# Unread products, count products and weight splits moved in the routing and last stages of a one-layer encoder

## The reference

```python
x = layer_norm(ALPHA * x + a, lp['ln1_g'], lp['ln1_b'])                       # a: token mixing
x = layer_norm(ALPHA * x + cross_attend(x, mk, mv, lp['w_xq'], lp['w_xo']), lp['ln2_g'], lp['ln2_b'])
x = layer_norm(ALPHA * x + hier_moe(x, lp), lp['ln3_g'], lp['ln3_b'])
...
def cross_attend(x, mk, mv, w_xq, w_xo):
    ...
    return o @ w_xo                                                            # the outward product
...
def hier_moe(x, lp):
    logits_g = (xt @ lp['w_router_group']).astype(jnp.float32) + lp['b_router_group'].astype(jnp.float32)
    ...
    top_v, top_i = lax.top_k(le, TOP_K)
    gate = (jax.nn.softmax(top_v, axis=-1) * pg[:, None]).reshape(-1)
    ...
    h = jax.nn.silu(xb @ w_g[e]) * (xb @ w_u[e])                               # one block of rows of expert e
    return (h @ w_d[e]) * wts[:, None].astype(xt.dtype)
```

## Time and profile before

| | us |
|---|---|
| median of 3 timed runs | 1626.03 |
| lowest, highest | 1622.83, 1627.28 |
| profiled execution | 1628.42 |
| its span (first to last instruction) | 1625.8 |
| PE busy | 1552.3 (95%) |
| DVE busy | 1005.0 (62%) |
| ACT busy | 787.0 (48%) |
| POOL busy | 362.8 (22%) |
| mean granted TensorE clock | 0.978 |

### The profile page before, as it was taken

How to read it: one execution, slowest core, us unless ns; L and a number is a source line. 1 busy time by engine, 2 the same in 40 slices (tenths; PEclk the granted TensorE clock), 3 DMA queues, 4 the chain that set the end, 5 groups by cost and what they waited for, 6 DMA issues and landing times.

```text
span 1625.8 us, 21437 instructions
## 1 busy us (share of the span) xinstructions
PE 1552.3 (95%) x8440; PEld 1279.9 (79%) x8440; DVE 1005.0 (62%) x1282; ACT 787.0 (48%) x1143; POOL 362.8 (22%) x277
## 2 busy tenths in 40 slices
PE   8999999999988999999999988999999999999966
PEld 6877887677766888999777777888888888888842
DVE  5611111777644655222555458989889998999936
ACT  5411121555454013222422234887888887888834
POOL 0000000477862851000122111131111121111005
PEclk9999999999999999999999977999999999999987
DMA  9721111600333545000445536999999999999876
GB/s 356 260 76 39 43 56 59 174 23 19 118 104 132 184 170 193 27 21 1 156 156 175 175 130 251 385 368 396 387 382 399 398 389 393 385 392 398 342 283 282
DMA packets 86331, 352.69 MB, mean 217 GB/s; under 512 B 23512, under 2 KB 28248, under 8 KB 64474
## 3 DMA queue, kind: packets, MB, share of 16 engines
q1 hardware_dynamic: 76106, 331.41, 54.1%
q0 software_dynamic: 9216, 18.89, 3.0%
q10 hardware_dynamic: 912, 1.05, 0.2%
HBM read 321.93 MB, written 43.15 MB: 225 GB/s over the span
## 4 chain that ended last, share of the span: by engine, by line
PE 85%; DVE 5%; DMA 4%; ACT 3%; issue 1%; POOL 0%; SPq 0%; DVEq 0%; POOLq 0%; ACTq 0%
PE M L1348 23%; PE M L1067 12%; PE T L862 6%; PE M L835 6%; PE T L1348 5%; PE T L771 3%; DMA beside<-in_w_exp_up 3%; DVE rounded L1905 3%; PE M L771 3%; PE M L950 2%; PE T L1409 2%; PE T L1139 2%; PE T L1137 2%; PE T L1138 2%; PE M L1171 2%; PE M L1153 2%
## 5 line engine op out<-in xcount | busy, mean ns | idle before, releaser
L1905 DVE TENSOR_TENSOR rounded<-beside,rounded 128x1024 fp32r<-128x1024 f32 (+1 forms) x397 | 471.4, 1233 | 57.2 <-ACT rounded L1791 46.7
L1348 PE MATMUL M<-rounded 128*128 128x512 f32 x1908 | 461.3, 392 | 2.8 <-ACT rounded L1826 1.9
L1348 PEld LDWEIGHTS M<-rounded 128*128 128x128 f32 x1908 | 355.8, 188 | 77.7 <-ACT rounded L1826 2.1
L1791 ACT CAST rounded<-beside 128x1024 fp32r<-128x1024 f32 x256 | 258.9, 1050 | 80.9 <-DMA beside<-in_w_exp_up 75.4
L1067 PE MATMUL M<-rounded 128*128 128x512 f32 x816 | 196.7, 395 | 2.9 <-ACT rounded L1661 1.7
L1067 PEld LDWEIGHTS M<-rounded 128*128 128x128 f32 x816 | 150.1, 188 | 33.9 <-issue 2.0
L1801 ACT CAST rounded<-beside 128x1024 fp32r<-128x1024 f32 x128 | 125.2, 1049 | 24.2 <-DMA beside<-in_w_exp_down 22.3
L2573 POOL DMA_INDIRECT expert_rows<-beside,route_out x32 | 41.8, 1305 | 394.8 <-ACT beside L1832 389.5
L2506 POOL TENSOR_SCALAR arena<-arena,rinv 128x384 f32<-128x384 f32 (+7 forms) x64 | 110.2, 1726 | 48.9 <-DVE rinv L2033 48.7
L1348 PE MATMUL T<-rounded 128*128 128x512 f32 x384 | 108.7, 398 | 0.0
L1905 DVE TENSOR_TENSOR rounded<-T,rounded 128x512 fp32r<-128x512 f32 (+2 forms) x84 | 79.0, 944 | 20.7 <-ACT rounded L1674 17.7
(11 more groups left out here) (374 smaller groups left out, 2462.4 us busy)
## 6 DMA issues: line engine op xcount, KB each, us to landing
beside<-in_w_exp_gate SPq DMA_DIRECT2D x64, 1024.0 KB, 8.1
beside<-in_w_exp_up SPq DMA_DIRECT2D x64, 1024.0 KB, 10.9
beside<-in_w_exp_down SPq DMA_DIRECT2D x32, 2048.0 KB, 11.4
arena<-x_rows SPq DMA_DIRECT2D x27, 512.0 KB, 3.7
x_rows<-arena SPq DMA_DIRECT2D x18, 512.0 KB, 3.1
arena<-expert_rows SPq DMA_DIRECT2D x9, 1024.0 KB, 12.7
arena<-in_x_prompt SPq DMA_DIRECT2D x16, 512.0 KB, 3.9
arena<-in_cache_mem_k SPq DMA_DIRECT2D x8, 1024.0 KB, 5.7
```

Of the source, the lines that this page charges most:

```text
L1348: got = nc.tensor.matmul(out, x[xs], (high, low)[ws](w)[:, c:c + 512], start=(first and n == 0), stop=(last and n == 2))
L1791: nc.scalar.copy(as_both(high(c)), both_raw(c)).then_inc(gu_high, 1)
L1905: return nc.vector.tensor_tensor(out, x, highs.bitcast(f32), ALU.subtract)
```

## The change

Six edits, all between the last outward product and the experts, and at the start of the last stage:

1. On PE the samples' outward product is cut into parts: `samples_high` (high rows by both weight parts) for four chunks of the first half ahead of `turn_x2(PT - 1)`, four behind it, the second half's behind `route_rows(PT - 1)`, and the low products (`samples_low`) last. `turn_memory_rows(NB - 1)` goes ahead of them. On ACT `turn_x2(PT - 1)` goes behind `out_high(PT)`. The samples' low part is made by DVE and no longer by POOL.
2. For the last prompt tile DVE adds the epsilon of the norm, and POOL only takes the inverse root.
3. DVE sums the eight pick tables into `picked` (the buffer of `r_end`), and one product each takes the place of the 16 count products; they stand behind later waits.
4. Nine unread f32 products (`ident` by `tables`, 512 columns) stand behind the ranks, four unread rounded ones behind the slot products, and 26 instead of 20 behind the totals.
5. The splits of the first expert's weights on DVE: chunk 0 goes behind the prompt tiles' slots, chunks 1 to 7 behind the routes. Before, chunk 0 stood ahead of the samples' first sum, 1 to 3 between the two sums, 4 to 7 behind the routes.
6. 26 unread f32 products (`ident` by `tables`, 512 columns) stand ahead of PE's wait in the last stage.

```diff
             weigh_memory_rows(NB - 1)
+            turn_memory_rows(NB - 1)
+            hi, lo = chunks(rows_hi[0]), chunks(rows_lo[0])
+
+            def samples_high(c, ks):
+                for k in ks:
+                    for part in (high, low):
+                        nc.tensor.matmul(M[0][:, c:c + 512], hi[k], part(k)[:, c:c + 512], start=(k == 0 and part is high), stop=False)
+
+            def samples_low(c, k):
+                return nc.tensor.matmul(M[0][:, c:c + 512], lo[k], high(k)[:, c:c + 512], start=False, stop=(k == KT - 1))
+
+            pe.wait_ge(rows_high, 3 * NT)
+            pe.wait_ge(logits_done, 2 + PT - 1)
+            samples_high(0, range(4))
             turn_x2(PT - 1)
-            turn_memory_rows(NB - 1)
+            samples_high(0, range(4, KT))
             route_rows(PT - 1)
-            pe.wait_ge(rows_high, 3 * NT)
+            samples_high(512, range(KT))
             pe.wait_ge(o_low, NT)
-            pe.wait_ge(logits_done, 2 + PT - 1)
-            hi, lo = chunks(rows_hi[0]), chunks(rows_lo[0])
-            for c in (0, 512):
-                for k in range(KT):
-                    for x, part in ((hi, high), (hi, low), (lo, high)):
...
+            for k in range(KT):
+                got = samples_low(0, k)
+            got.then_inc(product_ps, 1)
+            for k in range(KT):
+                samples_low(512, k).then_inc(w_used, 1)
...
-            for t in range(PT):
-                for counted in (ranks_last, totals):
-                    nc.tensor.matmul(counted, ones, picks[:, t * NE:(t + 1) * NE], start=(t == 0), stop=False)
+            for _ in range(9):
+                nc.tensor.matmul(M[1][:, 0:512], ident, tables[:, 0:512], start=True, stop=True)
             turn_x2(PT)
             route_rows(PT)
             pe.wait_ge(sel_ready, 1)
+            nc.tensor.matmul(ranks_last, ones, picked, start=True, stop=False)
...
+            for _ in range(4):
+                nc.tensor.matmul(M[0][:, 512:1024], sel_slot[:, 0, 0, :], sel_slot[:, 0, 0:4, :], start=True, stop=True)
             pe.wait_ge(softmax_in, 6)
...
+            nc.tensor.matmul(totals, ones, picked, start=True, stop=False)
             nc.tensor.matmul(totals, ones, picks[:, PT * NE:], start=False, stop=True).then_inc(rank_ps, 1)
-            for _ in range(20):
+            for _ in range(26):
                 nc.tensor.matmul(M[0][:, 0:512], sel_slot[:, 0, 0, :], sel_slot[:, 0, 0:4, :], start=True, stop=True)
...
+            for _ in range(26):
+                nc.tensor.matmul(T[0][:, 0:512], ident, tables[:, 0:512], start=True, stop=True)
             pe.wait_ge(wukT_ready, 2)
...
             memory_rows(NB - 1)
-            turn_x2(PT - 1)
             memory_rows_turned(NB - 1)
             act.wait_ge(sxo_done, NB)
             out_high(PT)
+            turn_x2(PT - 1)
...
+                    dve.wait_ge(rows_high, 2 * NT + PT + 1)
+                    nc.vector.tensor_tensor(rows_lo[0], oT[:, PT, :, :].rearrange("p k c -> p (k c)"), rows_hi[0].bitcast(f32),
+                                            ALU.subtract).then_inc(o_low, 1)
                     add_logits(PT - 1)
                     pick_experts(slice(0, PT), PT)
-                    split_gate_up(0, (0,))
...
-                    split_gate_up(0, (1, 2, 3))
...
+            nc.vector.tensor_reduce(picked, picks[:, 0:PT * NE].rearrange("p (t e) -> p e t", e=NE), AX.X, ALU.add)
             find_slots(slice(0, PT), PT, 0, sel_slot)
+            split_gate_up(0, (0,))
             add_logits(PT)
...
-            split_gate_up(0, range(4, KT))
+            split_gate_up(0, range(1, KT))
...
-            out_low(PT)
+            pool.wait_ge(var_ready, NT + PT)
+            nc.gpsimd.tensor_tensor(rstd[1][:, :], moments[1][:, 1:2], minus_half[:, 0:1], ALU.pow).then_inc(rstd_ready, 1)
```

More of the change, by code:

```diff
@@ L320, in encoder_layer_kernel @@
         r_count, r_over, r_end = (route(NE) for _ in range(3))
+        picked = r_end
         assert at[0] <= ARENA
@@ L1301, in _ @@
             weigh_memory_rows(NB - 1)
+            turn_memory_rows(NB - 1)
[9 more added lines that the diff above has]
+            samples_high(0, range(4))
             turn_x2(PT - 1)
-            turn_memory_rows(NB - 1)
+            samples_high(0, range(4, KT))
             route_rows(PT - 1)
-            pe.wait_ge(rows_high, 3 * NT)
+            samples_high(512, range(KT))
             pe.wait_ge(o_low, NT)
-            pe.wait_ge(logits_done, 2 + PT - 1)
-            hi, lo = chunks(rows_hi[0]), chunks(rows_lo[0])
-            for c in (0, 512):
-                for k in range(KT):
-                    for x, part in ((hi, high), (hi, low), (lo, high)):
-                        got = nc.tensor.matmul(M[0][:, c:c + 512], x[k], part(k)[:, c:c + 512], start=(k == 0 and x is hi and part is high),
-                                               stop=(k == KT - 1 and x is lo))
-                    if c > 0:
-                        got.then_inc(w_used, 1)
-                    elif k == KT - 1:
-                        got.then_inc(product_ps, 1)
+            for k in range(KT):
[3 more added lines that the diff above has]
+                samples_low(512, k).then_inc(w_used, 1)
             pe.wait_ge(softmax_in, 3)
@@ L2092, in add_rows @@
                 dve.sem_inc(waited, 1)
-                nc.vector.bn_aggr(moments[u][:, :], stats[u][:, :]).then_inc(var_ready, 1)
+                got = nc.vector.bn_aggr(moments[u][:, :], stats[u][:, :])
+                if n == NT + PT - 1:
+                    got.then_inc(dve_step, step.next())
+                    dve.wait_ge(dve_step, step.value())
+                    got = nc.vector.tensor_scalar(moments[u][:, 1:2], moments[u][:, 1:2], LN_EPS, None, ALU.add)
+                got.then_inc(var_ready, 1)
             def norm_rows(n, u, x, r, gain, shift):
@@ L2553, in _ @@
                     nc.gpsimd.memset(xg[1], 0.0)
-                deviation(NT + t, t % 2)
-            out_low(PT)
+                if t < PT - 1:
+                    deviation(NT + t, t % 2)
+            pool.wait_ge(var_ready, NT + PT)
+            nc.gpsimd.tensor_tensor(rstd[1][:, :], moments[1][:, 1:2], minus_half[:, 0:1], ALU.pow).then_inc(rstd_ready, 1)
             pool.wait_ge(var_ready, NT + PT + 1)
```

## The result

The changed kernel takes 1630.05 us in the median, the kernel before beside it 1625.95: a ratio of 1.0026, with a 95% interval from 1.0017 to 1.0035. Measured once more beside the experiments, it took 1627.86 against 1625.45, 1.0014 (1.0002 to 1.0025). The change costs 2 to 4 us, within 0.3%.

The account below looks back on a forecast made before the run. PE carries 85% of the chain, so steps count by PE's next start. Last stage 5.7 us lost minus routing stage 1.3 gained is 4.4 us more: 1632.8 us profiled, 1630.4 us timed, range 1625.5 to 1634.5.

Parts of the forecast that it names:

- Last stage, 5.7 lost: Last stage: 26 unread products outlast the 14.0 us gap, real products run at full clock; 5.7 us lost, ends 5.2 and 6.4.
- The rival that an unread product costs one record: Last stage: an unread f32 product costs 0.43 us, so 26 fit inside the gap; 1618 us, chance 0.03.
- Routing stage, 1.3 gained: Routing stage: routes 4.7 us earlier, block 1's hidden rows 1.3 us earlier; ends 3.0 gained, 1.1 lost.
- the clock ahead of the samples' product: Routing stage: clock has fallen when the samples' first products start at 946.0, and returns after 3.9 us of work, at 949.9.
- a clock that stays up: Rival, routing stage: full clock throughout, routes 2.5 us earlier still, about 3.8 gained in all; 1628 us, chance 0.09.
- Nine unread products, 3.3 us wasted: Behind the ranks: nine products keep PE until 971.9, though the samples' rows are ready at 968.6.
- Seven splits behind the routes: DVE behind the routes: seven splits instead of four, 3.45 us more; routes to block 1's first split 15.6 us without waiting.
- The 26 small unread products behind the routes: PE behind the routes: 26 instead of 20 end after the gather, but DVE is later still and hides that.
- The signs that I named: Wrong if last-stage unread products end before 1584, routes come before 981, or PE's start in block 1 does not follow DVE.
- The splits that eat the gain: Rival, routing stage: clock returns late, routes only 2.3 us earlier, block 1's weights 1.1 later; 1632.8 us, chance 0.43.
- the 6.4 as an end of the last stage: Last stage: upper end of the range given for the loss, around 5.7 us.
- routes at 985.0: Routing stage: routes ready at about 985.0, 4.7 us earlier than before.

Follow-up runs that it names:

- kernel with 15: Changed kernel with 15 instead of 26 unread f32 products in the last stage: 1621.5 us, ratio 0.9973 to the kernel before.
- the two products put ahead: Two more unread f32 products before PE's wait for the samples' rounded rows, against the kernel with 15 in the last stage and six behind the ranks: 1619.64 us.

## Why the prediction was right, and where it was not

Forecast were 4.4 us more; measured are 4.1 by the first comparison's medians and 2.4 by the second's. That the sum held is in part luck: the loss was a little too small and the gain too small by more, and the two errors go against each other.

**Last stage, 5.7 lost.** Right in mechanism and nearly in size: 52 records in 22.32 us (22.4 forecast), all real products at full clock (24.05, 24.1 forecast), 46.36 us from the experts' last product to PE's (46.5). The traces give 5.1 to 6.1, and about 7 where the experts' last products ran slow; the kernel before with these products alone gives 6.2 (4.1 to 8.3). The rival that an unread product costs one record falls with the 52.

**Routing stage, 1.3 gained.** Too small: the kernel without the last stage's products gains 2.4 by medians, 3.7 by the ratio. The step that failed is the clock ahead of the samples' product. I let it fall there, as at 945.28 in the kernel before, and gave a clock that stays up a chance of 0.09. In the two profiles of the changed kernel it stays up; so it does in four of the eight further profiles with the product by parts, and in the other four it falls. Where it falls, the order of the steps is the forecast's, but they come later. The kernel with 15 has its first eight products and the turn at half clock,

```profile
945.33 3.78 PE L1309 MATMUL M<-rounded 128*128 128x512 f32 x8 [1.43 <-ACT rounded L1756]
948.91 1.91 PE L772 MATMUL T<-tables,arena 128*128 128x128 f32 x8
```

and the clock comes back at 951.40, 6.07 us after the first of these products, where I had let it come back after 3.9:

```profile
950.00:951.00 1.00, 1.00 (x5) 0.94 (x4) 0.00 (x0) 0.15 (x1) 0.00 (x0) 0.50 0.78 287
951.00:952.00 1.00, 1.00 (x5) 0.79 (x4) 0.00 (x0) 0.86 (x1) 0.00 (x0) 0.80 1.06 451
```

In the table's count its samples' turn, router and routes come at 30.2, 32.3 and 43.3, forecast 29.4, 31.5 and 42.5 (985.0 - 942.46). Its hidden rows come at 68.3, and the prediction's 1.3 us earlier than 69.8 makes 68.5. That they agree is luck again: routes 0.8 too late, and a load of block 1 that took 11.06 us from SP's request to ACT (993.37 to 1004.43) instead of 11.87 before. In the kernel without the 26, whose code up to there is the same, the clock falls in front too, but falls again only behind the samples' router. Its hidden rows come at 66.7. So profiles of one and the same order in this stage gained 1.5, 3.1, 5.5 and 5.7 us at the hidden rows.

Where the clock stays up, that is more than the 3.8 that I gave this rival, for two reasons of about 1 us each. Routes came 8.2 us earlier than before and not 7.2 (4.7 and 2.5), and SP's request with them. And the load took 10.9 us from SP's request to ACT, where I kept the 11.84 of before. It still sets the hidden rows, as I had it: DVE has no idle time from the routes on until it waits 0.26 us at 1000.85 for the chunk that ACT rounds from this load. SP's request and ACT's start on what was loaded, by the timeline:

```profile
988.86 0.43 SPq L710 DMA_DIRECT2D beside<-in_w_exp_up  x1
```

```profile
999.77 1.05 ACT L1805 CAST rounded<-beside 128x1024 fp32r<-128x1024 f32 x1 [1.64 <-DMA beside<-in_w_exp_up]
```

The timed runs suggest a mixture. Of the 12 of the kernel without the 26, five take 1618.5 to 1621.6 us and seven 1623.0 to 1625.0, with a mean granted clock of 0.985 to 0.988 in the five and 0.983 to 0.986 in the seven. The profiled execution of the changed kernel, with 1627.05 us and 0.992, is the fourth fastest of its 18; the 14 behind it have 0.984 to 0.990. So its full clock may be the better case and not the usual one. But a mean doesn't tell in which stretch the clock fell, so this isn't shown.

**Nine unread products, 3.3 us wasted.** Right: PE turns the rows 3.5 us after they are ready, and six instead of nine are worth 2.2 us at the end. **Seven splits behind the routes.** Right: from routes to block 1's splits it is 15.5 us (980.52 to 995.98; forecast 15.6), and PE's wait for DVE is 1.21 instead of 0.81. From the routes to the hidden rows it is 24.9 us instead of 22.4, and as much with the splits moved alone. In front, their move saves 2.2 us at the routes beside the nine unread products (kernel with the splits put back), and 0.9 in the kernel before, where it is a net loss of 1.5 at the hidden rows. **The 26 small unread products behind the routes**: PE takes the gathered rows without a wait, DVE is later still (991.83), as forecast.

**The signs that I named.** I wrote that I would be wrong if routes came before 981. They came at 980.52, in a stage that began 1.12 us earlier than in the kernel before; by 1.12 later they would be at 981.6. For that execution the forecast of the routing stage was wrong, and the rival with the clock up was right.

**The splits that eat the gain** fall in every profile: no kernel with the product by parts has later hidden rows than the kernel before. The condition of this rival, a clock that comes back 5.95 us after the first product, was met in the kernel with 15 (6.07). Routes came 4.0 us earlier there, not 2.3, and the hidden rows 1.5 earlier and not 1.1 later.

Two figures of the prediction don't follow from its own sums, and neither decides anything: the 6.4 as an end of the last stage, where the sum gives 6.2, and routes at 985.0, where 977.2 + 7.6 + 0.5 gives 985.3.

## What to carry to other kernels

Unread products that bridge a wait must end before what is waited for is there: size them from the wait in the trace and the price of the form, here 15 of 0.86 us for 14.0 us and six instead of nine, which turned 2 to 4 us lost into 6 us gained. Most of that is the loss which ends: 15 beside none were worth 0.8 us by the traces, because the second tile's rows came no earlier. A step that follows a pause should be priced at both clock levels with a fair chance for each, and work moved from DVE to POOL be looked at for instructions with two inputs in SBUF beside it.

## What was not expected of the hardware

The same order in this stage, with the same idle times ahead (0.62 and 1.43 us), met either clock level at the samples' first products: 2.13 us for eight of them in the profile of the changed kernel, 3.78 in that of the kernel with 15, whose code there is the same. The stretch in which it fell, to set beside 944:945 above:

```profile
944.00:945.00 1.00, 0.00 (x0) 0.00 (x0) 0.93 (x2) 0.97 (x2) 0.55 (x1) 0.79 0.00 0
```

Also the experts' last 24 products, behind a wait of 1.92 us, took 5.73 us in most profiles and 7.28 to 7.35 in four. What decides it stays open; the two products put ahead didn't settle it.
